# Neighbourhood attention over 176 keys a block, with queries and keys stored column by column and values projected feature-major

## The reference, cut to what matters

```python
def _na(q, k, v, q_w, k_w, rel_bias, meta_bias):
    ...
    q = _rmsnorm(q.reshape(B, L, NA_HEADS, NA_HEAD_DIM), q_w)
    k = _rmsnorm(k.reshape(B, L, NA_HEADS, NA_HEAD_DIM), k_w)
    ...
    c0 = np.clip(cols - NA_WIN_C // 2, 0, GRID_W - NA_WIN_C)
    col_idx_np = c0[:, None] + np.arange(NA_WIN_C)[None, :]
    ...
        s_win = (jnp.einsum('bqhd,brqchd->bhqrc', q_row, k_win).astype(jnp.float32) * scale
                 + bias.astype(jnp.float32)[None])
        s_meta = jnp.einsum('bqhd,bmhd->bhqm', q_row, k_meta).astype(jnp.float32) * scale + meta_b
        s = jnp.concatenate([s_win.reshape(B, NA_HEADS, GRID_W, n_win), s_meta], axis=-1)
        p = jax.nn.softmax(s, axis=-1).astype(v.dtype)
```

## Time and profile before

| | |
|---|---|
| median of 3 runs | 1277.93 us (1277.87 to 1278.14) |
| the profiled execution | 1275.89 us, its span 1274.1 us |
| PE, DVE, ACT, POOL busy | 1239.2 (97%), 822.2, 658.6, 147.2 us |
| granted TensorE clock, mean | 0.995 |
| DMA | 210.89 MB, mean 166 GB/s |

### The profile page before, as it was taken

How to read it: one execution, slowest core, us unless ns; L and a number is a source line. 1 busy time by engine, 2 the same in 40 slices (tenths; PEclk the granted TensorE clock), 3 DMA queues, 4 the chain that set the end, 5 groups by cost and what they waited for, 6 DMA issues and landing times.

```text
span 1274.1 us, 27430 instructions
## 1 busy us (share of the span) xinstructions
PE 1239.2 (97%) x10074; PEld 1191.6 (94%) x10074; DVE 822.2 (65%) x1378; ACT 658.6 (52%) x1105; POOL 147.2 (12%) x209
## 2 busy tenths in 40 slices
PE   6999999999999999999999999999989989999998
PEld 6999999999999999999999999999978878987888
DVE  6667665867666655667656777667657666535664
ACT  6445543646544545445544555545445656644652
POOL 3000000351000000000001340000021000002540
PEclk9999999999999999999999999999998999999999
DMA  7555654345556644555644346556633320435442
GB/s 285 185 190 186 236 168 144 133 133 199 181 181 207 220 167 151 181 187 202 222 148 165 117 149 198 181 181 224 204 120 121 124 100 22 161 100 174 149 141 83
DMA packets 56197, 210.89 MB, mean 166 GB/s; under 512 B 6672, under 2 KB 8720, under 8 KB 56000
## 3 DMA queue, kind: packets, MB, share of 16 engines
q1 hardware_dynamic: 54048, 203.45, 47.1%
q0 software_dynamic: 1936, 6.47, 1.6%
q10 hardware_dynamic: 144, 0.06, 0.0%
HBM read 208.91 MB, written 1.05 MB: 165 GB/s over the span
## 4 chain that ended last, share of the span: by engine, by line
PE 92%; DVE 4%; ACT 2%; issue 2%; DMA 0%; POOL 0%; DVEq 0%; ACTq 0%; SPq 0%; POOLq 0%
PE bank L1064 27%; PE bank L1066 26%; PE bank L1065 26%; PE bank L1389 2%; DVE w_lo L676 2%; PE bank L1102 1%; PE bank L1372 1%; DVE h_lo L695 1%; PE bank L1359 1%; PE bank L1300 1%; PE bank L1302 1%; PE bank L1301 1%; ACT w_hi L408 1%; PE bank L1354 1%; PE bank L1157 0%
## 5 line engine op out<-in xcount | busy, mean ns | idle before, releaser
L1064 PE MATMUL bank<-h_hi,w_hi 128*128 128x256 f32 (+1 forms) x1992 | 570.3, 286 | 17.3 <-DVE w_lo L676 11.7
L1065 PE MATMUL bank<-h_lo,w_hi 128*128 128x256 f32 (+1 forms) x1992 | 563.0, 283 | 0.0
L1066 PE MATMUL bank<-h_hi,w_lo 128*128 128x256 f32 (+1 forms) x1992 | 562.7, 282 | 0.0
L676 DVE TENSOR_TENSOR w_lo<-w_raw,w_hi 128x1024 fp32r<-128x1024 f32 (+1 forms) x360 | 465.9, 1296 | 81.2 <-ACT w_hi L408 80.5
L408 ACT ACTIVATE w_hi<-w_raw 128x1024 fp32r<-128x1024 f32 (+1 forms) x360 | 397.8, 1109 | 91.8 <-PE bank L1066 68.3
L1064 PEld LDWEIGHTS bank<-h_hi,w_hi 128*128 128x128 f32 x1992 | 378.2, 190 | 27.4 <-issue 22.9
L1066 PEld LDWEIGHTS bank<-h_hi,w_lo 128*128 128x128 f32 x1992 | 379.0, 190 | 0.0
L1065 PEld LDWEIGHTS bank<-h_lo,w_hi 128*128 128x128 f32 x1992 | 376.5, 189 | 0.9
L1064 PE MATMUL bank<-g_hi,w_hi 128*128 128x256 f32 x832 | 230.4, 277 | 0.8 <-DVE x_res L861 0.8
L1065 PE MATMUL bank<-g_lo,w_hi 128*128 128x256 f32 x832 | 229.8, 276 | 0.0
L1066 PE MATMUL bank<-g_hi,w_lo 128*128 128x256 f32 x832 | 229.8, 276 | 0.0
(11 more groups left out here) (153 smaller groups left out, 1189.3 us busy)
## 6 DMA issues: line engine op xcount, KB each, us to landing
w_raw<-in_w SPq DMA_DIRECT2D x296, 512.0 KB, 3.3
w_raw<-in_wd SPq DMA_DIRECT2D x64, 704.0 KB, 4.1
rel_bias<-in_relbias POOLq DMA_DIRECT2D x32, 128.0 KB, 2.4
btab_sb<-in_btab POOLq DMA_DIRECT2D x1, 1536.0 KB, 9.6
x_res<-in_xT SPq DMA_DIRECT2D x2, 512.0 KB, 5.0
out_T<-x_res SPq DMA_DIRECT2D x8, 128.0 KB, 1.7
rope_sb<-in_rope POOLq DMA_DIRECT2D x1, 272.0 KB, 3.5
mats_sb<-in_mats POOLq DMA_DIRECT2D x1, 192.0 KB, 3.9
```

Of the source, the lines that this page charges most:

```text
L676: dve.tensor_tensor(wlo[:, slot, 0:cols], raw[:, slot, 0:cols], whi[:, slot, 0:cols].bitcast(F32), ALU.subtract).then_inc(lo_ready[slot], 1)
L1064: pe.matmul(o, h, xh, start=first, stop=False)
L1065: pe.matmul(o, h, xl, start=False, stop=False)
L1066: return pe.matmul(o, lo, xh, start=False, stop=last)
```

## The change

- Tokens of queries and keys are stored column by column of the grid (position 4 x column + row) instead of row by row. A block of 128 queries is then 32 columns, and its windows lie in 40 columns of keys. Keys are stored with the 16 meta keys on both sides (NK is 288), so that each block reads one run of 176 (`key_window`). DVE's scaling (L966) writes in this order; for keys it gets a second small instruction for the meta copies.
- Scores, bias addition, exponential and normalisation work on 176 keys instead of 272. The probabilities of a head are transposed in two tiles instead of three, and multiplied in two parts, one of 80 and one of 128 keys. The copy to `probs_T` is 256 columns instead of 384.
- Values are projected feature-major: 8 outputs of 128 features with 272 moving columns. ACT then copies each to `probs_T` in column order (`nav_copy`, two instructions), PE turns it by three transposes back into the same bank (`turn_values`), and DVE copies 3x128 columns to `v_heads`. The turning of value output j stands behind the run of output j+2 on PE.
- Waits of PE on `pj_taken` are set anew: before the fourth value bank, before the attention (20 outputs taken instead of all), before the first two fills and the first `values_of`.
- POOL loads the bias of a step with four DMAs of 32 partitions into unused columns of `w_raw`, one step ahead, then makes one copy and two additions over 160 columns, which read at a distance of 64 elements and write in order. It starts when the first attention has been transposed.

The diff, cut to the core:

```diff
+QC, KC = 32, 40
+KW = KC * WR
+NW = META + KW
+NK = META + T + META
+EDGE = META + 16 * WR
...
-    outs += [("nav", 3 * c + t, base + 16 + 4 * c + 3) for c in range(2) for t in range(3)]
+    outs += [("nav", 4 * c + f, base + 16 + 4 * c + 3) for c in range(2) for f in range(4)]
...
+            return bank[2 * (step % 2) + hh][:, 0:TM] if mla else bank[hh][:, 0:NW]
+
+        def key_window(b):
+
+            return slice(0, NW) if b == 0 else slice(NK - NW, NK)
+
+        def probs_window(v):
+
+            at = 0 if v % 4 < 2 else NK - NW - EDGE
+            return Prn[:, v % 4, at:at + NW]
+
+        def value_tiles(b):
+
+            return ((0, EDGE, 0), (1, P, EDGE)) if b == 0 else ((1, P, 0), (2, EDGE, P))
...
+            pool.wait_ge(tr_done, U0 + 2 * MH)
+            pool.memset(Prn[:, 0:2, NW:EDGE + P], 0.0)
+            pool.memset(Prn[:, 2:4, 0:NK - NW - EDGE], 0.0)
+
+            def load_bias(step):
+                p, b, s0 = step // 2, step % 2, 2 * (step % 2)
+                if step >= 2:
+                    pool.wait_ge(rel_ready, 2 * (step - 1))
+                for r in range(WR):
+                    t, c = r // 2, r % 2 * GW + QC * b
+                    src = relbias[2 * p:2 * p + 2, c:c + QC, 2 - 2 * t:6 - 2 * t, :].rearrange("h c r k -> c h (r k)")
+                    pool.dma_start(raw[r::WR, s0:s0 + 2, PT8:PT8 + T], src).then_inc(rel_loaded[b], 16)
+
+            load_bias(0)
             for step in range(NH):
-                t = step % 2
+                p, b, s0 = step // 2, step % 2, 2 * (step % 2)
+                two = slice(s0, s0 + 2)
+                if step + 1 < NH:
+                    load_bias(step + 1)
+                if step >= 2:
+                    pool.wait_ge(nm_done, U0 + 2 * MH + 2 * (step - 1))
+                at_meta, at = (0, META) if b == 0 else (KW, 0)
+                pool.tensor_copy(rel[:, two, at_meta:at_meta + META], metab[:, 2 * p:2 * p + 2, :])
+                pool.wait_ge(rel_loaded[b], 64 * (step // 2 + 1))
+                grid = raw[:, two, PT8:PT8 + T].rearrange("p h (r k) -> p h k r", r=WR)
+                k0 = (GW - KC) * b
                 for hh in range(2):
-                    i, h = 2 * step + hh, 2 * (step // 2) + hh
-                    if step >= 2:
-                        pool.wait_ge(nm_done, U0 + 2 * MH + i - 3)
-                    pool.dma_start(rel[:, i % 4, 0:T], relbias[h][:, 2 - 2 * t:6 - 2 * t, :].rearrange("p r c -> p (r c)"))\
-                        .then_inc(rel_loaded[i % 4], 16)
-                for hh in range(2):
-                    pool.tensor_copy(rel[:, (2 * step + hh) % 4, T:TM], metab[:, 2 * (step // 2) + hh, :])
-                for hh in range(2):
-                    i = 2 * step + hh
-                    pool.wait_ge(rel_loaded[i % 4], 16 * (i // 4 + 1))
-                    r4 = rel[:, i % 4, 0:T].rearrange("p (r c) -> p r c", r=4)
-                    pool.tensor_tensor(r4, r4, cmask[:].unsqueeze(1).broadcast_to([P, 4, GW]), ALU.add)\
-                        .then_inc(rel_ready, 1)
+                    mask = cmask[:, b].unsqueeze(2).broadcast_to([P, KC, WR])
+                    ins = pool.tensor_tensor(rel[:, s0 + hh, at:at + KW].rearrange("p (k r) -> p k r", r=WR),
+                                             grid[:, hh, k0:k0 + KC], mask, ALU.add)
+                    ins.then_inc(rel_ready, 1)
...
+            def nav_copy(outs, i):
+
+                j = outs[i][1]
+                if j >= 2:
+                    act.wait_ge(nav_turned, j - 1)
+                wait_output(act, outs, i)
+                b, dst = bank[out_bank(outs, i)], PT[:, j % 2]
+                act.activation(dst[:, META:META + T].rearrange("p (c r) -> p r c", r=WR),
+                               b[:, 0:T].rearrange("p (r c) -> p r c", r=WR), ACT.Copy)
+                act.activation(dst[:, 0:NK].rearrange("p (a m) -> p a m", m=META)[:, 0:NK // META:NK // META - 1],
+                               b[:, T:TM].unsqueeze(1).broadcast_to([P, 2, META]), ACT.Copy).then_inc(nav_copied, 1)
...
+                    if 0 <= n - LAG < len(outs) and outs[n - LAG][0] == "nav":
+                        nav_copy(outs, n - LAG)
...
+                            if kind == "naq":
+                                parts = [(qn[:, k].rearrange("p (c r) -> p r c", r=WR),
+                                          *(a[:, 0:T].rearrange("p (r c) -> p r c", r=WR)
+                                            for a in (bank[i % 4], rs[:, g % 2])))]
+                            elif kind == "nak":
+                                meta_out = kna[:, k].rearrange("p (a m) -> p a m", m=META)
+                                parts = [(kna[:, k, META:META + T].rearrange("p (c r) -> p r c", r=WR),
+                                          *(a[:, 0:T].rearrange("p (r c) -> p r c", r=WR)
+                                            for a in (bank[i % 4], rs[:, g % 2]))),
+                                         (meta_out[:, 0:NK // META:NK // META - 1],
+                                          *(a[:, T:TM].unsqueeze(1).broadcast_to([P, 2, META])
+                                            for a in (bank[i % 4], rs[:, g % 2])))]
+                            else:
+                                parts = [(normed_dst(kind, k, c), bank[i % 4][:, 0:nt], rs[:, g % 2, 0:nt])]
+                            for dst, src, rstd in parts:
+                                ins = dve.scalar_tensor_tensor(
+                                    out=dst, in0=src, scalar=sml[:, gain:gain + 1],
+                                    in1=rstd, op0=ALU.mult, op1=ALU.mult)
...
+                    i = n - LAG - 2
+                    if 0 <= i < len(outs) and outs[i][0] == "nav":
+                        j = outs[i][1]
+                        dve.wait_ge(nav_turned, j + 1)
+                        dve.tensor_copy(V[:, :, j * P:(j + 1) * P],
+                                        bank[out_bank(outs, i)][:, 0:3 * P].rearrange("p (t c) -> p t c", t=3))\
+                           .then_inc(pj_taken, 1)
...
+            def turn_values(outs, i):
+
+                j = outs[i][1]
+                pe.wait_ge(nav_copied, j + 1)
+                for n, at in enumerate((0, EDGE, EDGE + P)):
+                    tr = pe.transpose(bank[out_bank(outs, i)][:, n * P:(n + 1) * P], PT[:, j % 2, at:at + P], ident)
+                tr.then_inc(nav_turned, 1)
...
-                    tt = k % 3
-
-                    def values(kp_, tile):
+                    f = k % 4
+
+                    def values(kp_, ft):
                         s = (piece - 3 + kp_) % SLOTS
+                        b = bank[out_bank(outs, n - f + ft)][:, 0:TM]
                         for i in range(2):
-                            c = (2 * kp_ + i) * TM + KEYS[tile]
-                            b = bank[out_bank(outs, n - tt + tile)]
-                            wh, wl = whi[:, s, i * 512:(i + 1) * 512], wlo[:, s, i * 512:(i + 1) * 512]
-                            pe.matmul(b[:], hhi[:, c:c + P], wh, start=kp_ + i == 0, stop=False)
-                            pe.matmul(b[:], hlo[:, c:c + P], wh, start=False, stop=False)
-                            mm = pe.matmul(b[:], hhi[:, c:c + P], wl, start=False, stop=kp_ == 3 and i == 1)
+                            at = i * 512 + ft * P
+                            wh, wl = whi[:, s, at:at + P], wlo[:, s, at:at + P]
+                            xh, xl = hcols(2 * kp_ + i, TM)
+                            pe.matmul(b, wh, xh, start=kp_ + i == 0, stop=False)
+                            pe.matmul(b, wh, xl, start=False, stop=False)
+                            mm = pe.matmul(b, wl, xh, start=False, stop=kp_ == 3 and i == 1)
                         return mm
 
-                    if tt == 0:
+                    if f == 0:
                         for kp_ in range(3):
                             begin(piece - 3 + kp_)
-                            for tile in range(3):
-                                mm = values(kp_, tile)
+                            for ft in range(4):
+                                if kp_ == 0 and k == 0 and ft == 3:
+                                    pe.wait_ge(pj_taken, st_n0 + n - 2)
+                                mm = values(kp_, ft)
                             mm.then_inc(w_used[(piece - 3 + kp_) % SLOTS], 1)
                         begin(piece)
-                    mm = values(3, tt)
+                    mm = values(3, f)
...
-                            pe.wait_ge(pj_taken, st["n0"] + n - 3)
-                        run(outs, n)
+                            pe.wait_ge(pj_taken, st["n0"] + min(n - 3, 16 if outs is NA else n))
+                        run(outs, n, st["n0"])
+                    if outs is NA and 0 <= n - LAG - 1 < len(outs) and outs[n - LAG - 1][0] == "nav":
+                        turn_values(outs, n - LAG - 1)
...
-                        pe.matmul(o, qn[r, p, tok], kn[r, p, :], start=True, stop=True).then_inc(sc_done, 1)
```

(16 more changed lines are left out.)

72 lines of the change are left out of this document (40 added, 32 removed).

## The result

The changed kernel takes **1279.05 us** (median, 1276.49 to 1281.92), the kernel before beside it 1277.26 (1274.23 to 1278.14), ratio 1.0017 [1.0011, 1.0023]. Forecast were 1262.9 us, in a range of 1257.5 to 1269.0. The profiled execution took 1279.11 us with a span of 1277.3 and a mean clock of 0.993. It is 3.2 us longer than that of before.

The account below looks back on a forecast made before the run. PE was taken as the bound (92% of the chain that ended last). Value projections -4.5, attention steps -10.2 and last waits -0.3 sum to -15.0 us, from 1277.93 to a median of 1262.9 us; range 1257.5 to 1269.0.

Parts of the forecast that it names:

- signs of being wrong: Whole forecast: wrong if the attention step is over 4.9 or under 4.5 us, or the value stage over 33 or under 28.
- Value projections: First value product to first scores, second block: 31.3 us against 35.78, a gain of 4.5 us.
- The wait at the first turning: Value projections: PE waits about 3.1 us for ACT's first copy, which stands behind three splits.
- that of the last copy: End of the value projections: PE waits once more, about 0.6 us, for ACT's last copy.
- T + 5.0 less T + 2.0: First value turning: copy's end less PE's arrival, T being the moment of the last key output's sum; put at about 3.1 us.
- rival 3: First turning of values: clock falls to 0.50 in the stall, costing half of some 7 us, 1266.4 us; chance 0.04.
- ACT's strided copies: Value copies: 0.42 and 0.19 us; if distant writes took twice 0.42, the stage gains 3.7 us.
- The step: Second attention: 5.30 us becomes 4.66 (values -0.24, transposes -0.22, scores -0.18); 16 steps give -10.2 us.
- rival 2: Second attention's values: 80-row products do not run in pairs, so values gain nothing; 1266.7 us; chance 0.06.
- The last waits: End of the second attention: shorter copies of transposed probabilities cut two of the waits by 0.13 each, -0.3 us.
- rival 4: Second attention: POOL becomes the step's bound and the kernel gets slower, 1285.3 us at 1.9 us an addition; chance 0.05.
- DVE's key scaling: Key stage: second instruction and strided writes hide in DVE's 1.31 us wait ahead of a 0.50 us scaling; no cost.

Follow-up runs that it names:

- e5: The changed kernel with the column mask tile placed past all others and an unused 256-byte tile in its old place, restoring g and y; 1261.29 us, ratio 0.9876.
- e6: As e5, but ACT makes the three high parts behind the first value copies, one behind each, instead of ahead of them; 1260.74 us.
- e13: As e5, but first-block h tiles 1024 bytes apart, h and g both 192 bytes from the weights modulo 512; 1248.96 us, ratio 0.9801.
- e1: The kernel before with only an unused 64-byte tile ahead of g_hi; 1292.10 us, ratio 1.0119.
- e14: As e13, with ACT's order of e6 (three high parts behind the first value copies); 1244.45 us, ratio 0.9760.
- e16: As e13, but h at distance 64 from the weights modulo 512, g still at 192; 1264.1 us, single execution.
- e11: The kernel before with an unused 64-byte tile ahead of every tile, so weights, h and g all move; 1277.83 us, single execution.
- e9: As e5, but first-block h tiles 1024 instead of 1088 bytes apart and moved; h stood at distance 160, g at 224; 1274.73 us.
- e12: The changes of e9 and e6 together; 1272.64 us.
- e7: The kernel before with an unused 512-byte tile ahead of g_hi; 1278.04 us, single execution.

## Why the prediction was wrong

**The step that failed** is one that it did not take. The sum begins with the value projections and carries everything ahead of them over unchanged. Of the grown constants it costs only the DMA ("issued by POOL at the kernel's start"), and costs it at nothing. The mask tile grows from `[P, 64]` to `[P, 2, KC]`; that this moves g and y, and that products care, is missing: +14.7 us ahead of the second block and 2.1 us behind the first scores. The price of moving g stood in no row of before, since every g product there has one place. But the trace of before showed that the place counts: 0.355 and 0.340 us for equal triples of h and of g, and h triples that go from 0.353 to 0.357 with the tile. The prediction did not look for either, and its signs of being wrong (step, value stage) watch only the changed stages.

With the place restored (e5) the forecast stands: 1261.29 against 1262.9. That it comes so close is in part luck. The median lies between two executions at 1259.31 and 1259.71 us, with a mean clock of 0.996, and two at 1262.86 and 1264.27 with 0.993; and in the profiled one the span fell by 1274.1 - 1261.0 = 13.1 us, not by 15.0. The terms, by e5 and after:

- **Value projections**, forecast 31.3 us (-4.5): 32.6 (-3.2). The wait at the first turning was 2.82 us against 3.1 (the prediction's own T + 5.0 less T + 2.0 makes 3.0), that of the last copy 0.41 against 0.6. The stage lost 1.5 us to the clock, which is rival 3 in less than half its size (3.5 us there). e6 shows that this wait is what ACT's order makes it. e13 waits 2.83 us at the same place with the clock at 1.00 throughout, so the fall doesn't follow from the stall alone, and its stage takes 31.1 us, near the forecast 31.3. Windows of e13:

```profile
1113.10:1144.20 31.10, 27.85 (x220) 27.12 (x218) 14.51 (x19) 15.40 (x30) 0.00 (x0) 1.00 0.44 152
```

- **ACT's strided copies** were not dearer where it counts: one starts 0.40 us ahead of its small companion, which is the 0.42 of the sum; the record's length is 0.61. The Trainium skill (SBUF — State Buffer, "Door 1: The DMA port swizzle") speaks of a penalty; the trace has at most these 0.2 us of length, and none in the pitch.
- **The step**, forecast 4.66: 4.71 with h and 4.61 with y in e5. In the step of after shown above values take 0.60 against 0.57, transposes 0.58 as forecast, scores 0.50 against 0.49. The 80-row products run in pairs, which settles rival 2. First scores to the end: 110.65 to 100.74 us in e5, -9.9 against -10.5.
- **The last waits** were 1.05 and 0.53 us, 1.6 in all for the 1.9 of the earlier trace rows: the forecast 0.3 less.
- **POOL** (rival 4): an addition takes 0.594 us, inside 0.46 to 0.74. The Trainium skill (GPSIMD Engine Reference, "Performance pitfalls for Q7 kernels") has such reads at 50% more; here it is 3.71 ns a column against 2.89 in the earlier trace rows, 29% more, any fixed part included. The copy took 0.95 us where 0.2 to 0.4 were put. POOL's work is 4 x 0.558 + 0.95 + 2 x 0.594 = 4.37 us of a 4.7 us step: it came nearer to the bound than forecast, but no wait of PE goes back to it.
- **DVE's key scaling** takes 0.75 us for its two instructions in place of 0.50, and DVE still waits 1.32 us ahead of it, so the slack was there.

The chance of 0.94 for faster was too high because the rivals were all mechanisms of the changed lines. What a diff changes outside its stage, sizes of tiles and so the places of all behind them, had no share in the chances.

## What to carry to other kernels

A change that alters the size of a tile moves the tiles allocated behind it; read the true bytes of the built program before and after, and compare the pace of equal products in stages that nobody touched before crediting or blaming the edit. If the pace differs, a pad or a moved tile separates layout from logic in one run. A win of 1% can hide behind 1% of placement, and two groups of equal products with different paces in one trace are themselves an opening.

## What the runs showed of the hardware

- A product of 128x128 by 256 columns in fp32r, at the full clock, took 0.1133 us (0.340 a triple) to 0.120 us (0.360), on the same code, with the place of its moving tile 64 bytes apart (before and e1). By distance from the weights modulo 512: 0 0.360; 64 0.353; 128 0.356 to 0.360; 160 0.352 to 0.360; 192 0.340, in some stages 0.353 (e13, e14, e16, the tail of e6); 224 0.355; 256 0.360; 320 0.353 us a triple. 384 and 448 were only seen in the mean over eight. The pairs 0 and 256, 64 and 320, and the cycle of four h tiles in before agree with a period of 256 bytes.
- What in the chip does it is open. That it is the distance from the weights rests on e11, where all tiles moved together and g kept 0.340. No run separates the weights' read from the moving read, or varies the place of the high parts against that of the low ones (always equal here), and why one stage has 0.340 and the next 0.353 at the same bytes was not tried.
- In the profiled executions the granted clock fell to 0.5 for 3.4 us around the end of a 2.8 us stall (after, e5, e9), behind the short waits at the attention's end (e6, e12), and at neither (e13, e14), though e13 has the stall and both have the short waits. Removing the stall gave the profiled run of e6 1.1 us of the 3.5 that the stage gained; the medians of e5 and e6 differ by 0.6, inside the spread. A fall of the same length stands at the start of the second layer, near 480 us, in e6, e7, e9 and e11 to e14, and not in before, after or e5; what decides it is open.
